# Attention scores by 64-row halves of the array, without staged queries, and full tiles for the sample's own keys

## The reference, cut to what matters

```python
def diff_attend(q, q_pos, segments, lam):
    scale = HEAD_DIM ** -0.5
    scores = []
    for k, _, k_pos in segments:
        s = jnp.einsum('bqhmd,bkhmd->bhmqk', q, k).astype(jnp.float32) * scale
        visible = (k_pos[None, :] // CHUNK) <= (q_pos[:, None] // CHUNK)
        scores.append(jnp.where(visible, s, -1e30))
    p = jax.nn.softmax(jnp.concatenate(scores, axis=-1), axis=-1)
    p = p[:, :, 0] - lam * p[:, :, 1]
    out = 0.0
    start = 0
    for k, v, _ in segments:
        n = k.shape[1]
        out = out + jnp.einsum('bhqk,bkhe->bqhe', p[..., start:start + n].astype(v.dtype), v)
        start += n
    return out
```

## Time and profile before

| | |
|---|---|
| median of three runs | 2477.97 us |
| the profiled execution | 2473.48 us |
| its span, first to last instruction | 2471.6 us |
| mean granted TensorE clock | 0.970 of full speed |
| TensorE matmuls busy | 2344.1 us, 95% |
| its weight loads busy | 2270.5 us, 92% |
| DVE, ACT, POOL busy | 63%, 47%, 25% |

### The profile page before, as it was taken

How to read it: one execution, slowest core, us unless ns; L and a number is a source line. 1 busy time by engine, 2 the same in 40 slices (tenths; PEclk the granted TensorE clock), 3 DMA queues, 4 the chain that set the end, 5 groups by cost and what they waited for, 6 DMA issues and landing times. The chain is left out here.

```text
span 2471.6 us, 42451 instructions
## 1 busy us (share of the span) xinstructions
PE 2344.1 (95%) x16911; PEld 2270.5 (92%) x16911; DVE 1567.1 (63%) x2299; ACT 1150.9 (47%) x1933; POOL 629.4 (25%) x601
## 2 busy tenths in 40 slices
PE   8999999998987999999999999999989999889996
PEld 7989999998987999999999999999978888879995
DVE  4997769557799477444574585555685565475444
ACT  4345543454633656433354475445465454344332
POOL 3256401124200333111241231111342111151112
PEclk9999999898998999999999999999989999989998
DMA  9567665354754455645578655434554445345451
GB/s 228 155 180 223 194 210 166 103 165 125 211 173 144 131 172 146 186 145 149 167 215 238 180 167 162 128 112 129 153 157 130 120 137 171 107 117 161 146 149 59
DMA packets 702005, 390.06 MB, mean 158 GB/s; under 512 B 24969, under 2 KB 689010, under 8 KB 701810
## 3 DMA queue, kind: packets, MB, share of 16 engines
q1 hardware_dynamic: 649648, 328.77, 46.1%
q10 hardware_dynamic: 52162, 58.59, 7.4%
HBM read 365.48 MB, written 21.82 MB: 157 GB/s over the span
## 5 line engine op out<-in xcount | busy, mean ns | idle before, releaser
L469 PE MATMUL tile_ps<-xh,wh 128*128 128x256 f32 (+1 forms) x3584 | 1092.7, 305 | 45.8 <-POOL xl L719 26.4
L453 DVE TENSOR_TENSOR wl<-raw,wh 128x1024 fp32r<-128x1024 f32 (+1 forms) x640 | 793.9, 1241 | 503.6 <-ACT wh L447 502.1
L470 PE MATMUL tile_ps<-xl,wh 128*128 128x256 f32 (+1 forms) x3584 | 1072.5, 299 | 0.0
L471 PE MATMUL tile_ps<-xh,wl 128*128 128x256 f32 (+1 forms) x3584 | 1072.2, 299 | 0.0
L447 ACT CAST wh<-raw 128x1024 fp32r<-128x1024 f32 (+1 forms) x640 | 654.8, 1025 | 804.0 <-PE tile_ps L471 792.3
L469 PEld LDWEIGHTS tile_ps<-xh,wh 128*128 128x128 f32 x3584 | 690.7, 193 | 57.0 <-issue 23.6
L470 PEld LDWEIGHTS tile_ps<-xl,wh 128*128 128x128 f32 x3584 | 692.2, 193 | 1.1 <-issue 0.2
L471 PEld LDWEIGHTS tile_ps<-xh,wl 128*128 128x128 f32 x3584 | 691.5, 193 | 0.0
L580 POOL TENSOR_TENSOR hl<-hf,hh 128x256 fp32r<-128x256 f32 (+1 forms) x176 | 251.6, 1430 | 1208.6 <-ACT hh L510 1208.5
L469 PE MATMUL tile_ps<-hh,wh 128*128 128x256 f32 (+1 forms) x1408 | 426.9, 303 | 20.6 <-DVE wl L453 11.0
L470 PE MATMUL tile_ps<-hl,wh 128*128 128x256 f32 (+1 forms) x1408 | 417.0, 296 | 0.0
(11 more groups left out here) (263 smaller groups left out, 1867.3 us busy)
## 6 DMA issues: line engine op xcount, KB each, us to landing
raw<-in_ffn_w_in_dram SPq DMA_DIRECT2D x352, 512.0 KB, 3.9
raw<-in_ffn_w_out_dram SPq DMA_DIRECT2D x128, 448.0 KB, 3.5
raw<-in_ffn_w_out_dram SPq DMA_DIRECT2D x64, 512.0 KB, 3.8
raw<-in_ssm_w_glu_dram SPq DMA_DIRECT2D x32, 512.0 KB, 3.9
raw<-in_attn_w_kv_dram SPq DMA_DIRECT2D x32, 512.0 KB, 4.1
wt<-scr_w ACTq DMA_DIRECT2D x16, 512.0 KB, 4.0
cp<-scr_c ACTq DMA_DIRECT2D x16, 512.0 KB, 3.5
raw<-in_attn_w_q_dram SPq DMA_DIRECT2D x16, 512.0 KB, 3.9
```

Source lines behind the costliest of these rows:

```text
L453: nc.vector.tensor_tensor(wl[n % WS][:, 0:k, :], raw[n % RAWS][:, 0:k, :], wh[n % WS][:, 0:k, :].bitcast(F32), ALU.subtract).then_inc(w_lo, 1)
L469: nc.tensor.matmul(o, wh[w][:, kk, :], xa, start=kk == 0, stop=False)
L470: nc.tensor.matmul(o, wh[w][:, kk, :], xb, start=False, stop=False)
L471: mm = nc.tensor.matmul(o, wl[w][:, kk, :], xa, start=False, stop=kk == ROWS[n] - 1)
```

## The change

1. `scores` no longer reads `qs` but the queries where they lie: map m is a matmul over its own 64 rows, 0 to 63 or 64 to 127, of `qT` and `kT`. The keys go in chunks of at most 256, and inside a chunk first map 0, then map 1. It waits for the rotated queries of its head (`s_rope`) in place of the staging.
2. The mask is a matrix `mask` of 128 partitions, zeros except for rows 0 and 64, so that each map's mask contracts over the same 64 rows as its scores; both masks come after both maps' scores.
3. `pool_stage` is gone, with `qs`, its 4 memsets and 64 copies. `pool_stage_s`, which clears and fills `qd`, begins 30 steps into the FFN.
4. For the sample, `exS` has 128 own columns, the last 64 cleared by DVE once; `vtok` of the sample is cleared in partitions 64 to 127, by one DVE memset of 64x1024. The matmuls of the own keys turn 128 columns and contract over 128 rows. `exS` lies where the prompt's values were, so its clearing waits for the last prompt output (`s_o`).

```diff
@@ -222,7 +222,7 @@
         wh = [keep(f"wh{s}", [P, KMAX, P], F32R) for s in range(WS)]
         wl = [keep(f"wl{s}", [P, KMAX, P], F32R) for s in range(WS)]
         ones = keep("ones", [P, P])
-        maskrow = keep("maskrow", [1, P + CHUNK], F32R)
+        mask = keep("mask", [P, P + CHUNK], F32R)
         ident = keep("ident", [P, P])
         vec = keep("vec", [P, P])
         small = keep("small", [P, 16])
@@ -317,19 +317,16 @@
         xa = Map(x_at)
         ex = [[xa(f"ex0_{s}", [P, 2, 2 * P]) for s in range(2)]]
         pT = [[xa(f"pT0_{s}", [P, 2 * P]) for s in range(2)]]
-        qs = [[xa(f"qs0_{s}", [P, 2, P]) for s in range(2)]]
         assert xa.at <= x_at + 4 * DT * NT[0]
         junk = [Map(xl_at)("junk0", [P, P])]
         xa = Map(x_at + 4 * DT * NT[0])
         ex.append([xa(f"ex1_{s}", [P, 2, SEQ]) for s in range(2)])
-        qs.append([xa(f"qs1_{s}", [P, 2, P]) for s in range(2)])
         assert xa.at <= xl_at
         xa = Map(xl_at + 4 * DT * NT[0])
         pT.append([xa(f"pT1_{s}", [P, SEQ]) for s in range(2)])
         assert xa.at <= x_end
         otok = Map(rows_at)("otok", [P, 2, D])
         otok_s = Map(cos_at)("otok_s", [DEC, D])
-
 
 
         xa = Map(vt_at)
@@ -340,10 +337,8 @@
         xa = Map(qa_at)
         cv = [xa(f"cv{s}", [P, PAST // P, P]) for s in range(2)]
         assert xa.at <= qa_at + 4 * NH * NT[0]
-        xa = Map(ln_at)
-        exS = [xa(f"exS{s}", [P, PAST + DEC]) for s in range(2)]
-        assert xa.at <= ln_end
         xa = Map(v_at)
+        exS = [xa(f"exS{s}", [P, PAST + P]) for s in range(2)]
         pTS = [xa(f"pTS{s}", [P, (PAST // P + 1) * DEC]) for s in range(2)]
         assert xa.at <= v_at + 4 * 4 * D
 
@@ -562,13 +557,11 @@
             wait(pool, x_ready[0], lows_issued[0])
             wait(pool, x_ready[1], lows_issued[1])
 
-        qs_issued, qd_issued = [0], [0]
-        s_qs = sem("queries_staged")
+        qd_issued = [0]
         z_qs = sem("sample_queries_staged")
 
         def after_halves(pool):
             wait(pool, s_c, halves_issued[0])
-            wait(pool, s_qs, qs_issued[0])
             wait(pool, z_qs, qd_issued[0])
 
         def pool_in(pool, f, h, p, beside=None):
@@ -885,9 +878,10 @@
                 yield from idle(3)
             dve.wait_ge(s_cm, 4)
             V.tensor_scalar(cmat[:, 2], cmat[:, 1], -1.0, None, ALU.mult).then_inc(s_cm, 1)
-            V.memset(maskrow[:, 0:CHUNK].bitcast(F32), 1.0)
-            V.memset(maskrow[:, CHUNK:P].bitcast(F32), 0.0)
-            V.memset(maskrow[:, P:P + CHUNK].bitcast(F32), -1e30).then_inc(s_pad, 1)
+            link(dve, V.memset(mask[:, :].bitcast(F32), 0.0))
+            for m in (0, 64):
+                V.memset(mask[m:m + 1, 0:CHUNK].bitcast(F32), 1.0)
+                V.memset(mask[m:m + 1, P:P + CHUNK].bitcast(F32), -1e30).then_inc(s_pad, 1)
             yield
 
         def v_exp(dve, out, x_, a, b, c, kint=kint[:, :]):
@@ -1707,7 +1701,7 @@
         s_o = sem("pv_done")
         s_oe = sem("o_copied")
         s_sq = sem("o_squares_summed")
-        s_zq = sem("qs_cleared")
+        s_zq = sem("sample_queries_cleared")
         v_mx = sem("v_stats")
         v_rc = sem("v_reciprocals")
 
@@ -1741,33 +1735,13 @@
 
             return misc[:, 3 if it + 1 < 2 * ITEMS else 2, 0:P]
 
-        def pool_stage(pool, part):
-
-            pool.wait_ge(tile_done, FIRST["q", part] + NH)
+        def pool_stage_s(pool):
+
+            pool.wait_ge(s_vc, 5)
             after_whole(pool)
-            if part:
-                pool.wait_ge(s_vc, 5)
             for b in range(2):
-                nc.gpsimd.memset(qs[part][b][:].rearrange("p a b -> p (a b)"), 0.0).then_inc(s_zq, 1)
-                if part:
-                    nc.gpsimd.memset(qd[b][:, :], 0.0).then_inc(s_zq, 1)
-            pool.wait_ge(s_zq, 6 if part else 2)
-            for k in range(ITEMS):
-                it = part * ITEMS + k
-                i, h = ITEM[it]
-                pool.wait_ge(s_rope, (2 + part) * NH + h + 1)
-                wait(pool, s_sc, it - 1)
-                after_whole(pool)
-                c = i % 2 * P
-                for m in range(2):
-                    nc.gpsimd.tensor_copy(qs[part][it % 2][64 * m:64 * m + 64, m, :],
-                                          qT[part][64 * m:64 * m + 64, h, c:c + P]).then_inc(s_qs, 1)
-                qs_issued[0] += 2
-                if k:
-                    yield from idle(2)
-            yield
-
-        def pool_stage_s(pool):
+                nc.gpsimd.memset(qd[b][:, :], 0.0).then_inc(s_zq, 1)
+            pool.wait_ge(s_zq, 2)
             for h in range(NH):
                 pool.wait_ge(s_rope, 4 * NH)
                 wait(pool, z_own, h - 1)
@@ -1786,18 +1760,23 @@
 
             def scores(it):
                 i, h = ITEM[it]
-                b, kn = it % 2, (i + 1) * P
-                pe.wait_ge(s_qs, 2 * it + 2)
+                kn = (i + 1) * P
+                pe.wait_ge(s_rope, (2 + part) * NH + h + 1)
                 if it == 0:
                     pe.wait_ge(s_kc, 5)
                 elif it == ITEMS:
                     pe.wait_ge(s_vc, 5)
                 else:
                     pe.wait_ge(s_exp, 2 * it)
+                halves = (slice(0, 64), slice(64, P))
+                for c in range(0, kn, 2 * P):
+                    end = min(c + 2 * P, kn)
+                    for m in range(2):
+                        nc.tensor.matmul(misc[:, m, c:end], qT[part][halves[m], h, i % 2 * P:i % 2 * P + P],
+                                         kT[halves[m], h, c:end], start=True, stop=False, skip_group_check=True)
                 for m in range(2):
-                    nc.tensor.matmul(misc[:, m, 0:kn], qs[part][b][:, m, :], kT[:, h, 0:kn], start=True, stop=False)
-                    mm = nc.tensor.matmul(misc[:, m, kn - CHUNK:kn], maskrow[0:1, 0:P], maskrow[0:1, P:P + CHUNK],
-                                          start=False, stop=True)
+                    mm = nc.tensor.matmul(misc[:, m, kn - CHUNK:kn], mask[halves[m], 0:P], mask[halves[m], P:P + CHUNK],
+                                          start=False, stop=True, skip_group_check=True)
                 mm.then_inc(s_sc, 1)
 
             def transposes(it):
@@ -1995,7 +1974,7 @@
                 for kt in range(PAST // P):
                     nc.tensor.matmul(misc[:, 2, kt * DEC:(kt + 1) * DEC], exS[b][:, kt * P:(kt + 1) * P], dw[b][:, :],
                                      start=True, stop=True, skip_group_check=True)
-                nc.tensor.matmul(misc[0:DEC, 3, DEC:2 * DEC], exS[b][:, PAST:PAST + DEC], dw[b][:, :],
+                nc.tensor.matmul(misc[:, 3, DEC:2 * DEC], exS[b][:, PAST:PAST + P], dw[b][:, :],
                                  start=True, stop=True, skip_group_check=True).then_inc(z_pt, 1)
 
             def output(h):
@@ -2006,7 +1985,7 @@
                 for kt in range(PAST // P):
                     nc.tensor.matmul(misc[0:DEC, 3, P:2 * P], pTS[b][:, kt * DEC:(kt + 1) * DEC], cv[b][:, kt, :],
                                      start=kt == 0, stop=False, skip_group_check=True)
-                nc.tensor.matmul(misc[0:DEC, 3, P:2 * P], pTS[b][0:DEC, PAST // P * DEC:], vtok[0:DEC, 4, h * P:(h + 1) * P],
+                nc.tensor.matmul(misc[0:DEC, 3, P:2 * P], pTS[b][:, PAST // P * DEC:], vtok[:, 4, h * P:(h + 1) * P],
                                  start=False, stop=True, skip_group_check=True).then_inc(z_o, 1)
 
             for k in range(NH + 1):
@@ -2032,6 +2011,7 @@
         def dve_sample(dve):
             V = nc.vector
             V.tensor_tensor(fold[:, :], ident[:, 0:DEC], ident[:, DEC:P], ALU.add).then_inc(z_fold, 1)
+            V.memset(vtok[DEC:P, 4, :], 0.0)
 
             def maxima(h):
                 st = stz[:, h % 2]
@@ -2062,6 +2042,11 @@
                 if k < NH:
                     maxima(k)
                 yield
+                if k == 0:
+
+                    dve.wait_ge(s_o, 2 * ITEMS)
+                    for b in range(2):
+                        V.memset(exS[b][:, PAST + DEC:], 0.0)
                 if k == 1:
                     yield from dve_norms(dve, 1)
                 else:
@@ -2108,7 +2093,7 @@
                 act.wait_ge(z_pt, h + 1)
                 wait(act, z_o, h - 1)
                 A.copy(pTS[b][:, 0:PAST // P * DEC], misc[:, 2, :]).then_inc(z_ptc, 1)
-                A.copy(pTS[b][0:DEC, PAST // P * DEC:], misc[0:DEC, 3, DEC:2 * DEC]).then_inc(z_ptc, 1)
+                A.copy(pTS[b][:, PAST // P * DEC:], misc[:, 3, DEC:2 * DEC]).then_inc(z_ptc, 1)
 
             def evict(h):
                 act.wait_ge(z_o, h + 1)
@@ -2184,9 +2169,7 @@
             return chained(act_items(act, 0), act_roots(act, 0), idle(3), ends())
 
         def pool_attn(pool, part):
-            if part:
-                return chained(pool_stage(pool, 1), pool_stage_s(pool))
-            return pool_stage(pool, 0)
```

(1 more changed line is left out.)

## The result

The kernel after takes 2439.54 us (median of four runs, 2439.1 to 2440.83), the kernel before, timed beside it, 2477.82 us (2475.79 to 2480.94). The ratio is 0.9843, with a 95% interval of 0.9829 to 0.9857: 38 us faster, 35 to 42 by the interval. The forecast was 2457.4 us with a range of 2446 to 2470.

What follows compares the result with a forecast made beforehand. TensorE was taken to bound the kernel. Scores and masks 16.3, staging 1.0, clock 1.0 and sample 2.3 sum to 20.6 us saved, from a median of 2478.0 to 2457.4 us; range 2446 to 2470.

Steps and rivals of the forecast that it cites:

- TensorE bounds the stretch: In the two stretches of the items TensorE alone sets the end; a microsecond off its stream is one off the time.
- A border costs 0.20 us: Each switch between 128-row and 1-row matmuls costs 0.20 us; an item goes from four borders to two, 0.40 us.
- The scores: Scores and masks of the items, borders included: 7.65 us a head becomes 5.61, 16.3 us saved over 8 heads.
- middle model: Items' scores: loads one row ahead, both groups may work at once, second map one load later; 16.3 us saved, chance 0.52.
- Rival 1: Items' scores: full overlap, loads running ahead into the idle group; 21.5 us saved in place of 16.3, 2452.2 us, chance 0.18.
- Both ends that I worked out: Bounds on the scores' saving: 9.9 us with no overlap but hidden loads, 21.5 us with loads running ahead.
- Rivals 2 to 4: Scores: no overlap, 2463.8 us (0.14); loads lie open, 2474 us (0.08); row-group changes cost 0.20 us each, 2486.9 us (0.08).
- Staging: TensorE's wait on `qs` before the first item of part 1 goes: 1.0 us saved.
- Sample: The sample's own keys in 128-row form: turning saves 1.2 us, output 1.1 us, together 2.3; bounds 0 to 4.
- DVE's and POOL's work: DVE's added clearing and wait, and POOL's dropped copies and memsets, count nothing; 1.0 us if the clearing's cover is gone.
- The clock: First item of part 1, at half clock: full clock may return sooner and saved columns count more; 1.0 us of 0 to 2.3.

Runs made afterwards that it cites:

- full_mask: The kernel before with its mask as a matrix over all 128 rows, zeros but for one, so no border is left: 2455.93 us, ratio 0.9928.
- same_group: The kernel after with both maps' products on rows 0 to 63, map 0's scores computed twice and map 1's left out: 2464.84 us, ratio 0.9951.
- paired: The kernel after with the scores of two items issued together at every fourth step in part 0, DVE's maxima waiting for both: 2438.59 us, ratio 0.9852.
- chunk128: The kernel after with the keys in pieces of 128 in place of 256: 2442.96 us, ratio 0.9862 to the kernel before.
- scores_only: The kernel before with scores by 64-row halves and the 64-row masks, but staging into qs and the sample kept as before: 2443.35 us, ratio 0.9878.
- unchunked: The kernel after with all keys of an item in one matmul for each map: 2441.4 us, ratio 0.9858 to the kernel before.
- map_major: The kernel after with all pieces of map 0 written before those of map 1: 2441.01 us, ratio 0.9856 to the kernel before.
- major64: The kernel after with pieces of 64 keys, all of map 0's before map 1's: 2490.33 us in one run, beside 2475.65 before.

## Why the prediction was right and wrong

**TensorE bounds the stretch: right.** What its stream lost came off the time, microsecond for microsecond. DVE, ACT, POOL and the exponentials stood in no new wait of a score.

**A border costs 0.20 us: right.** 0.194 measured alone; `full_mask` and `same_group` come out with it to a few hundredths of a us an item, `paired` to 0.08 a pair.

**The scores: wrong, and this is the whole miss.** The step that failed is "I take the middle model because the rows show loads one ahead and no further", with its start "one load later" for the second map. Inside one row group loads do run one row ahead in the traces after as well; but the model also gave both groups one common line of loads and starts, and there is none. The second map's first row starts 7 ns behind the first map's, not 0.32 us. The traces give a simpler sum. An item costs the columns of one map, the mask's 0.03 and two borders of 0.20. With two rows of 0.106 us per 128 keys that is 0.64, 0.85, 1.07 and 1.28 us for 128 to 512 keys. Measured with the way in and out (0.19 more than the totals above): 0.65, 0.85, 1.08 and 1.28. The second map is free. The middle model had 4.01 us a head between the borders, the traces have 2.25: 1.76 a head, 14 us in all, the distance between the 16.3 us of the forecast and the 30.5 that the items gave (1.48 a head in part 0, 2.33 in part 1).

Rival 1, full overlap, was not far enough either. It let the second map start with the first map's second row, three steps where there are two, and had the loads come one after another, at 0.11. `chunk128` shows a pair of loads at the pace of one. Both ends that I worked out rested on the program's order of starts, and of loads, within one engine; the rows of before never had two row groups at work, so they could show nothing of it. The bound should have been the free second map: 3.85 a head, 30 us, which is what an idle array half can give at most, and the range's lower end would then have been about 2437. The prediction did quote the Trainium skill (TensorEngine Tiling, Key Properties) that tiles of one mode load and multiply independently. Here the traces agree fully, loads too, with rows and loads 7 ns apart, and that gives 30 us, not the 21.5 put beside it.

**Rivals 2 to 4: refuted.** No overlap is what `same_group` takes, 0.9951, not the kernel after. Loads don't lie open inside a row group (0.112 us a row). A change of row group costs nothing: pairs are 7 ns apart, the two one-row masks 4 ns.

**Staging: 1.0 us forecast, 0.95 measured** in the stage of the wait; whether it also lengthened the half clock by the 1.0 us of `scores_only` is open. **Sample: 2.3 forecast, 2.3 measured**; turning gave 0.15 to 0.18 a head, output 0.14. **DVE's and POOL's work: nothing, as forecast.**

**The clock: 1.0 us forecast, and not settled.** The first item of part 1 gained 2.54 us, its like at full clock 1.36: so 1.2 us more, because what was taken away ran at half clock, while the stretch at 0.51 did not become shorter. What ends that stretch was not tried, and it is not the change alone: the kernel after, run again, has 0.50 for 6.8 us, full clock for 3.4 and 0.50 for 3.4 more, `unchunked` 13.7 us at 0.50, `same_group` 20.5. It makes up to 1.3 us of difference in part 1 between kernels whose items at full clock are alike, more than this term is worth.

The sum by these terms is 30.5 + 1.2 + 1.0 + 2.3 = 35.0 us, beside 34.3 in the profiled pair and 38 of the medians. The rest of the medians is no larger than the spread in the start of the first item, but no trace shows that it lies there.

## What to carry to other kernels

Two products that contract over 64 rows each belong in the two row groups of the array, not in products padded with zeros: the second one, its weight loads included, cost nothing here as long as it stood within about four matmul rows of the first in the program. Each map wrote its own bank of `misc` in all these kernels; one bank for both was not tried. Since starts leave the program's order between row groups, a semaphore on the last matmul alone deserves a thought: here the second map's mask carries it, and whether it always ends last was not tested. Neighbours should have the same array form, small helpers like a mask too: a change of the row count costs 0.20 us, so gather what has an odd form and price it by the number of changes. Where a trace has never shown a resource at work, bound its gain by the resource itself (half the array is idle), not by the pace of the part that was in use.

## What the runs showed of the hardware

- Two row groups of 64 run side by side in matmuls and in weight loads: starts 6 to 7 ns apart (13 in `map_major`), pairs of loads 0.112 us apart where one group alone has 0.112 for each.
- Matmul rows start out of the program's order across row groups, up to about four rows ahead; what lies beyond runs alone (`major64`, 3.40 us for an item of 1.09).
- One change of form: 0.194 us.
- Behind a mask of the same form a little is left at the seam. In `full_mask` the second map's second score row starts 0.30 us after its first (256 keys), where the first map's takes 0.22; in `paired` it is 0.19 in place of 0.11. These 0.08 us are what a weight load (0.11) takes longer than the mask's columns (0.03); whether that is the cause was not tested.
- Programs that are the same, or nearly, up to the first item reach it between 1542.0 and 1547.3 us.
- The granted clock at part 1's first item came back to full between 0.5 us (`unchunked`) and 9.0 us (`same_group`) after its first score row; what decides it is open.
